# Products of the next panel issued at six norm joints in place of unread products

## The chip, the cores and the metric

The kernel runs on one core of a Trainium2 chip. The metric is the device time of one execution in microseconds; the median of several executions is given. TensorE (PE in the profile) multiplies, VectorE (DVE) and ScalarE (ACT) do elementwise work, SyncE (SP) issues the transfers.

## The reference

Two stacks of transformer blocks on 256 rows of width 1024, in 32-bit floats. What matters here is the sequence of sublayers, each followed by a norm of its 256 x 1024 result, which the next sublayer multiplies by its first weights:

```python
def rmsnorm(x, w):
    y = xf * lax.rsqrt(jnp.mean(xf * xf, axis=-1, keepdims=True) + NORM_EPS)
...
        x = x + hybrid_mixer(rmsnorm(x, norm_mix_w[l]), w_in[l], ...
        x = x + memory_cross_attention(rmsnorm(x, norm_xa_w[l]), rmsnorm(mem, norm_mem_w[l]),
                                       xa_wq[l], xa_wkv[l], xa_wo[l])
        x = x + peer_ffn(rmsnorm(x, norm_ffn_w[l]), peer_wq[l], peer_sub_keys[l], peer_u[l], peer_v[l])
    return rmsnorm(x, norm_final_w)
...
def post_norm(x, sub, g, b):
    return layer_norm(DN_ALPHA * x + sub, g, b)

def swiglu(x, w1, w3, w2):
    return (jax.nn.silu(x @ w1) * (x @ w3)) @ w2
```

The second stack runs, each with a post_norm behind it: swiglu 0, spatial gating, swiglu 2, (keys and values for later, no norm), swiglu 3, sparse attention, swiglu 5.

## The kernel before

**Tiling.** The 256 rows are two row tiles of 128 (`TILES`). Weights stream in slots of 128 x 2048 through a ring of three; a column slot is a panel of 1024 inputs by 256 outputs, held as eight chunks (`DC`) of 128 inputs. Each operand is split into a high part in fp32r (`ScalarE`, a copy) and a low part, the rest (`VectorE`), and a product is three products: high by high, high by low, low by high. Activations stand transposed in `k.xT` (`x_transposed`): chunk by chunk, 128 inputs by 256 rows, with a high and a low plane. A panel is worked off in two halves `j` of 128 outputs: the weights of a chunk and half are the stationary operand, the 256 rows of `k.xT` the moving one.

**A joint with a norm.** The last products of a sublayer end row tile 0 first. `PostNorm` (layer norm, L2684) and `RmsNorm` (L2898) then take each row tile through the same steps: VectorE adds the residual, ScalarE squares with an accumulated sum (L2771, L2955) and takes the root (L2774, L2957), VectorE scales (L2754, L2938) and TensorE turns the tile in eight transposes (`turn_chunks`, L575), two PSUM banks of four; ScalarE writes each bank as high part (`high`, L404) and VectorE the low part (`low`, L409). Signal `highed` counts the high parts: 2 once tile 0 is there, 4 once tile 1 is.

Between the transposes of tile 0 and those of tile 1 TensorE has nothing that is needed. `stand_in` (L581, L584) fills that time with products of the identity by itself that nobody reads: in `RmsNorm.tensor` 4, then 6 once tile 1 is added, then 4 once `rooted` says its root is taken; in `PostNorm.tensor` 3, 7 and 4. After them come the transposes of tile 1: in the same block of the program where a block ends there (`last`, followed by 8 more stand-ins), or, passed on as `turn`, at the head of the next sublayer.

**The next panel.** `high_first` (L341) issues a first panel's products so that those with the rows' high parts come first: after the transposes of tile 1 it waits for `highed` 3, runs the first four chunks of both halves over all 256 rows (L356 with the weights' high part, L359 with their low part), waits for `highed` 4, runs the other four, waits for the low parts and runs the last sixteen (L389). The first slot of the next sublayer is split ahead by `Beginning`, so its weights are there while the norm runs.

**The six joints** are named here by letter: A, the RMS norm before the memory queries (`panels`); B, the RMS norm before the peer queries, where a block ends inside the joint and tile 1 is turned behind it (`TurnedBehind`); C, spatial gating into swiglu 2, a block ends behind the turned tile 1, and swiglu 2 begins with full 512-column products over high and low plane (L3107) and 256-column ones (L3108); D, swiglu 2 into the keys and values; E, swiglu 3 into the attention's queries, a block ends as in C, and `queries` uses `passes` (L398 to L400); F, attention output into swiglu 5.

Order is that of the code: each engine runs its own list and waits only where a semaphore wait is written.

Of the kernel before, what the change touches and what calls it, by code (L numbers as in the profile page):

```python
# [23 lines left out]
ALU = mybir.AluOpType  # L24
# [287 lines left out]
class Before:  # L312


    def __init__(self, splits_eaten, highed=None, written=None, banks_read=(), parts=None, turn=None, ahead=0):
        self.splits_eaten, self.highed, self.written, self.banks_read = splits_eaten, highed, written, banks_read
        self.parts, self.turn, self.ahead = parts, turn, ahead
        self.waited = 0
# [11 lines left out]
    def part(self, pe, m, i):  # L330
# [5 lines left out]
        if value > self.waited:  # L336
            self.waited = value
            pe.wait_ge(self.written[0], value)


def high_first(pe, before, out, operands, x_on_right, apart=False):  # L341
# [22 lines left out]
    if before.turn is None:  # L364
# [47 lines left out]
class Program:  # L412


    def __init__(self, nc, ctx, a):
# [5 lines left out]
        self.before = None  # L421
        self.gains_free = None
# [213 lines left out]
class TurnedBehind:  # L636
# [20 lines left out]
    def before(self):  # L657
        return Before((self.highed, 2), (self.highed, 2), (self.written, 4 - self.lows_from), turn=self.turn, ahead=2)
# [1551 lines left out]
def pick_and_run_experts(k, room):  # L2210
# [8 lines left out]
    with ExitStack() as ctx, k.stage() as block:  # L2219
# [37 lines left out]
        def _(pe):  # L2257
            def panel(m):
# [12 lines left out]
                if m == 0:  # L2271
                    ins = high_first(pe, behind.before(), out, operands, True)
# [411 lines left out]
class PostNorm:  # L2684
# [4 lines left out]
    def __init__(self, k, ctx, split, gains, which, slots, final=False, squares=None, last=False):  # L2689
# [6 lines left out]
        self.begin = None if final else Beginning(k)  # L2696
        self.gains_free = k.gains_free
# [82 lines left out]
    def ends(self):  # L2780

        self.k.before = Before((self.tile_done, 2 * TILES), (self.highed, 4), (self.written, 4), ((self.written, 1),),
                               turn=self.turn_last)
        self.k.gains_free = self.normed

# [3 lines left out]
    def tensor(self, pe):  # L2789
        if self.begin:  # L2790
            turn_chunks(pe, self.k, self.k.x[:, 0, :], 0, self.banks, 4, self.normed)
            stand_in(pe, self.k, 3)
            if self.which != 0:
# [4 lines left out]
            if self.last:  # L2798
                self.turn_last(pe, range(DC))
                stand_in(pe, self.k, 8)  # L2800
# [40 lines left out]
def out_and_norm(k, aT, slots, gains, which, ahead=None):  # L2841


    with ExitStack() as ctx, k.stage() as block:
# [3 lines left out]
        norm = PostNorm(k, ctx, split, gains, which, slots)  # L2848
# [49 lines left out]
class RmsNorm:  # L2898
# [5 lines left out]
    def __init__(self, k, ctx, split, gain, gain_landed, slots, begin, rows):  # L2904
# [7 lines left out]
        self.begin = Beginning(k, None if begin is True else begin)  # L2912
        self.same = begin is True
# [36 lines left out]
    def scalar(self, act):  # L2950
# [13 lines left out]
        self.high(act, 0)  # L2964
        squares(1)
        for b in range(1, 4 if self.same else 2):
# [5 lines left out]
    def tensor(self, pe):  # L2972
        turn_chunks(pe, self.k, self.rows[0], 0, self.banks, 4, self.normed)
        stand_in(pe, self.k, 4)
        pe.wait_ge(self.added, 2)
        stand_in(pe, self.k, 6)
        pe.wait_ge(self.rooted, 2)
        stand_in(pe, self.k, 4)

    def ends(self):  # L2980

        self.k.before = Before((self.tile_done, TILES), (self.highed, 4), (self.written, 4), ((self.written, 1),),
                               turn=self.turn_last)
# [58 lines left out]
def swiglu(k, gains, which, final=False, compress=None):  # L3042
# [10 lines left out]
    with ExitStack() as ctx, k.stage() as block:  # L3053
# [7 lines left out]
        norm = PostNorm(k, ctx, split, gains, which, 3 * UNITS, final, last=compress is not None)  # L3061
# [18 lines left out]
        def bank(u, n):  # L3080

            return 2 * n + (0 if u == 0 and split.before and not compress else 4)
# [4 lines left out]
        def up(pe, u, i):  # L3087
            for n in range(2):
# [12 lines left out]
                if u == 0 and n == 0 and split.before:  # L3101
                    ins = high_first(pe, split.before, out, operands, True, True)
                else:
# [1106 lines left out]
```

## Time and profile before

| | us |
|---|---|
| median of 3 runs | 2235.57 |
| lowest, highest | 2235.31, 2238.03 |
| span of the profiled execution | 2233.5 |
| TensorE busy in it | 2197.0 (98%) |
| VectorE, ScalarE busy | 1568.6 (70%), 1170.0 (52%) |

The profile is of one execution; for it the page gives the span, from the first to the last instruction, and no separate device time. The median of the runs is 2.1 us above this span. TensorE is busy almost all of the span, but busy counts the unread products of the joints as well, so at a joint one has to read what ends the time before the next needed product. Duration in a row is not spacing: products overlap, and the spacing of n equal ones is their common length less one duration, by n - 1.

### The profile page before, as it was taken

Reading aid. Unit: us, or ns where it says so; the run is one execution under the profiler, and the core shown is the slowest. Engines: PE = TensorE matmul, PEld = TensorE weight load, DVE = VectorE, ACT = ScalarE, POOL = GpSimd, SP = SyncE. Lnnn points to the kernel's source line nnn. Section 1 sums busy time; section 2 is a strip of 40 time slices with the busy share of each in tenths; the row PEclk is TensorE's granted clock in tenths of the full one; section 3 lists DMA queues with packets and bytes.
Section 4 is the critical chain, followed back from the end, with each engine's and each line's share of the span. In section 5 each row is a group of like instructions: output and inputs, shape, how many; then the busy total and the mean of one; then the engine's idle time right before and its main releaser. Section 6 shows DMA issues by size and latency. Waiting matters only on the chain. (4 is left out here: it accounts for less than half of the span.)

```text
span 2233.5 us, 37259 instructions
## 1 busy us (share of the span) xinstructions
PE 2197.0 (98%) x14678; PEld 1964.0 (88%) x14678; DVE 1568.6 (70%) x2935; ACT 1170.0 (52%) x2008; POOL 33.9 (2%) x20
## 2 busy tenths in 40 slices
PE   8999999999999999999999999999999999999998
PEld 8987889999999998888888889988889788888887
DVE  7975659999889976666666557766657465776655
ACT  6643454555554455565555455545544544585544
POOL 0100000010000000000000000000000000000000
PEclk9999999999999999999999999999999999999999
DMA  7418425555444456666655556536455655404552
GB/s 275 151 46 189 170 93 174 181 178 170 144 150 143 150 171 192 194 194 193 194 189 212 190 190 240 191 127 232 176 200 191 248 186 192 175 34 175 184 204 97
DMA packets 78310, 389.98 MB, mean 175 GB/s; under 512 B 9771, under 2 KB 12715, under 8 KB 49868
## 3 DMA queue, kind: packets, MB, share of 16 engines
q1 hardware_dynamic: 76684, 383.33, 49.3%
q0 software_dynamic: 1040, 4.19, 1.5%
q8 instruction: 106, 1.74, 0.3%
q14 instruction: 48, 0.39, 0.1%
q10 hardware_dynamic: 432, 0.33, 0.0%
HBM read 382.57 MB, written 5.24 MB: 174 GB/s over the span
## 5 line engine op out<-in xcount | busy, mean ns | idle before, releaser
L256 DVE TENSOR_TENSOR split_slots<-ring,split_slots 128x1024 fp32r<-128x1024 f32 x402 | 475.3, 1227 | 118.4 <-ACT split_slots L247 118.2
L247 ACT ACTIVATE split_slots<-ring 128x1024 fp32r<-128x1024 f32 x402 | 402.3, 1054 | 149.3 <-PE banks L400 123.3
L3107 PE MATMUL banks<-x_transposed,split_slots 128*128 128x512 f32 x1360 | 478.4, 395 | 0.3 <-PEq L464 0.3
L409 DVE SCALAR_TENSOR_TENSOR expert_lo<-ring,expert_hi 128x512 fp32r<-128x512 f32 x512 | 353.4, 697 | 165.7 <-ACT expert_hi L404 164.6
L404 ACT ACTIVATE expert_hi<-ring 128x512 fp32r<-128x512 f32 x512 | 324.0, 634 | 252.5 <-PE banks L400 252.5
L3108 PE MATMUL banks<-x_transposed,split_slots 128*128 128x256 f32 x1360 | 381.5, 281 | 0.0
L3107 PEld LDWEIGHTS banks<-x_transposed,split_slots 128*128 128x128 f32 x1360 | 255.3, 188 | 60.4 <-issue 0.5
L398 PE MATMUL banks<-x_transposed,expert_hi 128*128 128x256 f32 x1024 | 293.9, 287 | 2.5 <-DVE expert_lo L409 2.5
L399 PE MATMUL banks<-x_transposed,expert_hi 128*128 128x256 f32 x1024 | 287.8, 281 | 0.0
L400 PE MATMUL banks<-x_transposed,expert_lo 128*128 128x256 f32 x1024 | 287.7, 281 | 0.0
L3108 PEld LDWEIGHTS banks<-x_transposed,split_slots 128*128 128x128 f32 x1360 | 256.4, 189 | 1.5
L400 PE MATMUL banks<-expert_hi,weighted_split 128*128 128x512 f32 x512 | 199.2, 389 | 0.0
L398 PE MATMUL banks<-expert_hi,weighted_split 128*128 128x512 f32 x512 | 199.2, 389 | 0.0
L399 PE MATMUL banks<-expert_lo,weighted_split 128*128 128x512 f32 x512 | 199.2, 389 | 0.0
L3206 DVE TENSOR_TENSOR gate_and_value<-banks,products_with_low_parts 128x512 f32<-128x512 f32 x88 | 60.8, 691 | 195.8 <-ACT products_with_low_parts L3162 195.8
L398 PEld LDWEIGHTS banks<-x_transposed,expert_hi 128*128 128x128 f32 x1024 | 193.1, 189 | 3.8 <-DVE expert_lo L409 3.2
L399 PEld LDWEIGHTS banks<-x_transposed,expert_hi 128*128 128x128 f32 x1024 | 193.1, 189 | 0.0
L400 PEld LDWEIGHTS banks<-x_transposed,expert_lo 128*128 128x128 f32 x1024 | 193.0, 189 | 0.0
L3162 ACT ACTIVATE products_with_low_parts<-banks 128x512 f32<-128x512 f32 x88 | 52.6, 598 | 237.4 <-PE banks L3108 233.8
L398 PE MATMUL banks<-x_transposed,split_slots 128*128 128x256 f32 x544 | 154.1, 283 | 0.3 <-PEq L464 0.3
L399 PE MATMUL banks<-x_transposed,split_slots 128*128 128x256 f32 x544 | 152.7, 281 | 0.0
L400 PE MATMUL banks<-x_transposed,split_slots 128*128 128x256 f32 x544 | 152.7, 281 | 0.0
(491 smaller groups left out, 4020.5 us busy)
## 6 DMA issues: line engine op xcount, KB each, us to landing
ring<-in_ffn_w SPq DMA_DIRECT2D x132, 1024.0 KB, 4.8
ring<-in_peer_u SPq DMA_DIRECT2D x128, 512.0 KB, 3.5
ring<-in_peer_v SPq DMA_DIRECT2D x128, 512.0 KB, 3.6
ring<-in_w_in SPq DMA_DIRECT2D x16, 1024.0 KB, 6.0
ring<-in_sgu_w_in SPq DMA_DIRECT2D x16, 1024.0 KB, 4.8
ring<-in_peer_wq SPq DMA_DIRECT2D x8, 1024.0 KB, 7.3
ring<-in_sgu_w_out SPq DMA_DIRECT2D x8, 1024.0 KB, 4.9
ring<-in_kv_w SPq DMA_DIRECT2D x6, 1024.0 KB, 4.8
```

Of the source, the lines that this page charges most:

```text
L247: act.activation(self.parts[:, b, 0, p], self.k.w.slot(g)[:, p], ACT.Copy).then_inc(self.high_done, 1)
L256: ins = dve.tensor_tensor(self.parts[:, b, 1, p], self.k.w.slot(g)[:, p], self.parts[:, b, 0, p].bitcast(F32), ALU.subtract)
L398: pe.matmul(out, lh, rh, start=start, stop=False)
L399: pe.matmul(out, lh, rl, start=False, stop=False)
L400: return pe.matmul(out, ll, rh, start=False, stop=stop)
L404: return act.activation(dst, src, ACT.Copy, scale=scale)
L409: return dve.scalar_tensor_tensor(dst, src, scale, hi.bitcast(F32), ALU.mult, ALU.subtract)
L3107: pe.matmul(out(j, slice(0, 2 * SEQ)), lh, k.xT.both[:, c, :, :], start=(c == 0), stop=False)
L3108: ins = pe.matmul(out(j), ll, rh, start=False, stop=(c == DC - 1))
L3162: act.activation(rest[:, n, :, :], sums(u, n, 1), ACT.Copy).then_inc(copied[n], 1)
L3206: dve.tensor_tensor(whole[:, n, :, :], sums(u, n, 0), rest[:, n, :, :], ALU.add).then_inc(joined[n], 1)
```

## The change

A new class `TileAhead` issues products of the next panel for one row tile: for both halves and the asked chunks the weights' high part and low part by the 128 columns of the tile's high part. At each joint, behind the transposes of tile 0 and the first stand-ins (4 in `RmsNorm`, 3 in `PostNorm`), TensorE now waits for the panel's split weights and `highed` 1, issues 16 such products, waits for `highed` 2 and issues 16 more; then it waits for `rooted` 2 and issues 4 stand-ins. The other stand-ins there (6 and 7) are gone. After the transposes of tile 1 the next sublayer issues the same 32 products for tile 1 (A, B, D, F in `high_first`, E in `queries`) where 32 products of 256 columns stood, and at C each pair of 512 and 256 columns becomes one of 384 and one of 128. In `RmsNorm.scalar` the high part of bank 1 moves ahead of the squares of tile 1.

In the core of the diff below the arguments that hand `TileAhead` on (`k.ahead`, `begun`, `apart`) are partly left out.

```diff
+class TileAhead:
...
+    def ready(self, pe):
+        g = self.begin.g
+        pe.wait_ge(self.k.w.used[g % RING], g // RING + 1)
+
+    def products(self, pe, i, chunks=range(DC)):
...
+        rows = slice(i * P, (i + 1) * P)
+        for j in range(2):
+            bank, at = (j, i * P) if self.apart else (0, j * SEQ + i * P)
+            own = slice(j * P, (j + 1) * P)
+            for c in chunks:
+                first = i == 0 and c == 0 and (j == 0 or self.apart)
+                out = k.psum[:, bank, at:at + P]
+                pe.matmul(out, wh[:, c, own], k.xT.hi[:, c, rows], start=first, stop=False)
+                pe.matmul(out, wl[:, c, own], k.xT.hi[:, c, rows], start=False, stop=False)
@@ high_first
-    if before.turn is None:
+    if before.begun:
+        before.turn(pe, near)
+        before.turn(pe, far)
+        pe.wait_ge(before.highed[0], 3 - before.ahead)
+        before.begun.products(pe, 1, near)
+        pe.wait_ge(before.highed[0], 4 - before.ahead)
+        before.begun.products(pe, 1, far)
+    elif before.turn is None:
@@ PostNorm.tensor
             stand_in(pe, self.k, 3)
-            if self.which != 0:
+            if self.ahead:
+                self.ahead.ready(pe)
+                pe.wait_ge(self.highed, 1)
+                self.ahead.products(pe, 0, range(DC // 2))
+                pe.wait_ge(self.highed, 2)
+                self.ahead.products(pe, 0, range(DC // 2, DC))
+                pe.wait_ge(self.rooted, 2)
+                stand_in(pe, self.k, 4, 7)
+            elif self.which != 0:
                 pe.wait_ge(self.negated, 2 * TILES)
                 stand_in(pe, self.k, 7)
@@ RmsNorm.scalar
         self.high(act, 0)
+        self.high(act, 1)
         squares(1)
-        for b in range(1, 4 if self.same else 2):
+        for b in range(2, 4 if self.same else 2):
@@ swiglu, u == 0 and n == 0
+                elif u == 0 and n == 0 and ahead:
+                    rest = k.xT.both.rearrange("p c q n -> p c (q n)")[:, :, P:2 * SEQ]
...
+                            pe.matmul(out(j, slice(P, 2 * SEQ)), lh, rest[:, c, :], start=False, stop=False)
+                            ins = pe.matmul(out(j, slice(P, SEQ)), ll, rh[:, P:SEQ], start=False, stop=(c == DC - 1))
@@ queries
+            if m == 0:
+                ahead.products(pe, 1)
...
+                    if m == 0:
+                        ins = pe.matmul(k.psum[:, 0, j * SEQ:(j + 1) * SEQ], wh[:, c, own], k.xT.lo[:, c, :], start=False,
+                                        stop=(j == 1 and c == DC - 1))
```

In the orders below `split_slots` is the weights' split parts, `x_transposed` is `k.xT`, `ident` the identity, and a bracket names the semaphores that an instruction waits for. TensorE at joint D before, from the end of tile 0's transposes:

```order
L584 MATMUL banks<-ident 128x128 x3
L584 MATMUL banks<-ident 128x128 [waits stage_odd_13]
L584 MATMUL banks<-ident 128x128 x6
L584 MATMUL banks<-ident 128x128 [waits stage_odd_15]
L584 MATMUL banks<-ident 128x128 x3
L3589 UNCONDITIONAL_BRANCH
L575 MATMUL banks<-ident,x_natural 128x128 [waits stage_odd_18,slot_used_2]
L575 MATMUL banks<-ident,x_natural 128x128 x3
L575 MATMUL banks<-ident,x_natural 128x128 [waits stage_odd_18]
L575 MATMUL banks<-ident,x_natural 128x128 x3
L356 MATMUL banks<-x_transposed,split_slots 128x256 [waits stage_odd_20,stage_odd_21]
L359 MATMUL banks<-x_transposed,split_slots 128x256
```

The same place after the change; lines L365 and L366 alternate, 32 times in the first stretch and 32 in the second:

```order
L620 MATMUL banks<-ident 128x128 x3
L365 MATMUL banks<-x_transposed,split_slots 128x128 [waits stage_odd_20,slot_used_2]
L366 MATMUL banks<-x_transposed,split_slots 128x128
...
L365 MATMUL banks<-x_transposed,split_slots 128x128 [waits stage_odd_20]
...
L620 MATMUL banks<-ident 128x128 [waits stage_odd_15]
L620 MATMUL banks<-ident 128x128 x3
L3651 UNCONDITIONAL_BRANCH
L611 MATMUL banks<-ident,x_natural 128x128 [waits stage_odd_18,slot_used_2]
...
L365 MATMUL banks<-x_transposed,split_slots 128x128 [waits stage_odd_20]
...
L424 MATMUL banks<-x_transposed,split_slots 128x256 [waits stage_odd_21]
```

Seven stand-ins that waited for the mean of tile 1 have become 32 products of 128 columns, ahead of the transposes of tile 1; the products behind those transposes are as many as before, 32, and half as wide.

ScalarE at joint A before, from the squares of tile 0:

```order
L2955 ACTIVATE normed_rows,row_stats<-x_natural 128x1024 [waits stage_even_9]
L2957 ACTIVATE row_stats<-row_stats,epsilons 128x1 [waits stage_even_10]
L404 ACTIVATE x_transposed<-banks 128x4x128 [waits stage_even_14]
L2955 ACTIVATE normed_rows,row_stats<-x_natural 128x1024 [waits stage_even_9]
L2957 ACTIVATE row_stats<-row_stats,epsilons 128x1 [waits stage_even_10]
L404 ACTIVATE x_transposed<-banks 128x4x128 [waits stage_even_14] x3
```

and after:

```order
L3003 ACTIVATE normed_rows,row_stats<-x_natural 128x1024 [waits stage_even_9]
L3005 ACTIVATE row_stats<-row_stats,epsilons 128x1 [waits stage_even_10]
L439 ACTIVATE x_transposed<-banks 128x4x128 [waits stage_even_14] x2
L3003 ACTIVATE normed_rows,row_stats<-x_natural 128x1024 [waits stage_even_9]
L3005 ACTIVATE row_stats<-row_stats,epsilons 128x1 [waits stage_even_10]
L439 ACTIVATE x_transposed<-banks 128x4x128 [waits stage_even_14] x2
```

One high part has moved ahead of the squares of tile 1.

## Rows read from the trace of the kernel before

**Rows 1.** Busy times; waits of TensorE: us, times, longest us.
```profile
PE 2197.0 (98%) x14678; PEld 1964.0 (88%) x14678; DVE 1568.6 (70%) x2935; ACT 1170.0 (52%) x2008; POOL 33.9 (2%) x20
PE banks L356 <- ACT x_transposed L404: 1.0, 5, 0.2
PE banks L584 <- DVE norm_stats L2745: 0.9, 4, 0.3
```

**Rows 2.** Timeline of TensorE, joint D: start us, length us, engine, line, work.
```profile
1688.71 1.04 PE L575 MATMUL banks<-ident,x_natural 128*128 128x128 f32 x8
1689.58 0.83 PE L584 MATMUL banks<-ident 128*128 128x128 f32 x6
1690.64 2.76 PE L584 MATMUL banks<-ident 128*128 128x128 f32 x22 [0.23 <-DVE norm_stats L2745]
1693.40 1.23 PE L575 MATMUL banks<-ident,x_natural 128*128 128x128 f32 x8
1694.81 0.36 PE L356 MATMUL banks<-x_transposed,split_slots 128*128 128x256 f32 x1 [0.18 <-ACT x_transposed L404]
```

**Rows 3.** Stand-ins (L584) by window, A to F: first stand-in : first transpose, length, busy.
```profile
258.01:261.20 3.19, 3.19 (x28) 1.00 0.00 0
326.34:330.97 4.63, 3.29 (x28) 1.00 0.00 0
1496.68:1500.44 3.76, 3.50 (x28) 1.00 0.00 0
1689.58:1693.40 3.82, 3.59 (x28) 1.00 0.00 0
1932.54:1936.27 3.73, 3.50 (x28) 1.00 0.00 0
2037.28:2041.03 3.75, 3.59 (x28) 1.00 0.00 0
```

**Rows 4.** Timeline of TensorE: spacing of 512-column, 256-column and identity products.
```profile
900.05 0.39 PE L398 MATMUL banks<-expert_hi,weighted_split 128*128 128x512 f32 x1
...
901.87 0.39 PE L400 MATMUL banks<-expert_hi,weighted_split 128*128 128x512 f32 x1
...
336.18 2.06 PE L389 MATMUL banks<-x_transposed,split_slots 128*128 128x256 f32 x16
338.07 0.28 PE L398 MATMUL banks<-x_transposed,split_slots 128*128 128x256 f32 x1
...
326.34 3.29 PE L584 MATMUL banks<-ident 128*128 128x128 f32 x28
```

**Rows 5.** Weight loads by shape: line, stationary partitions * columns, count, busy us, mean ns.
```profile
L359 PEld LDWEIGHTS banks<-x_transposed,split_slots 128*128 128x128 f32 x112 | 21.1, 189 | 0.0
L400 PEld LDWEIGHTS banks<-x_transposed,narrow_split 128*48 128x48 f32 x8 | 1.0, 122 | 0.0
L400 PEld LDWEIGHTS banks<-x_transposed,gate_panel_split 128*16 128x16 f32 x8 | 0.8, 95 | 0.2
```

**Rows 6.** Timelines of weight loads and products, 117.5 to 118.5 us: 16 and 32 columns.
```profile
117.69 0.30 PEld L1037 LDWEIGHTS banks<-log_alpha_f,constants_sb 128*128 128x128 f32 x2
117.91 0.30 PEld L1038 LDWEIGHTS banks<-log_alpha_f,constants_sb 128*128 128x128 f32 x2
118.14 0.30 PEld L1039 LDWEIGHTS banks<-log_by_half,ones 128*128 128x128 f32 x2
...
117.80 0.29 PE L1037 MATMUL banks<-log_alpha_f,constants_sb 128*128 128x16 f32 x2
```

**Rows 7.** Timeline of ScalarE and VectorE, joint B.
```profile
326.11 0.60 ACT L404 ACTIVATE x_transposed<-banks 128x512 fp32r<-128x512 f32 x1 [3.30 <-PE banks L575]
326.93 1.06 ACT L2955 ACTIVATE first_blocks<-x_natural 128x1024 f32<-128x1024 f32 x1 [0.23 <-DVE x_natural L2930]
...
329.97 0.68 DVE L409 SCALAR_TENSOR_TENSOR x_transposed<-banks,x_transposed 128x512 fp32r<-128x512 f32 x1
```

**Rows 8.** Timeline of TensorE, behind joints C and E.
```profile
1501.59 1.95 PE L584 MATMUL banks<-ident 128*128 128x128 f32 x16
1503.84 0.47 PE L3107 MATMUL banks<-x_transposed,split_slots 128*128 128x512 f32 x1 [0.30 <-PEq L464]
...
1946.29 0.32 PE L398 MATMUL banks<-x_transposed,narrow_split 128*48 128x256 f32 x1 [0.71 <-DVE narrow_split L409]
```

More of the change, by code:

```diff
@@ L421, in __init__ @@
         self.before = None
+        self.ahead = None
         self.gains_free = None
@@ L655, in lows, with before @@
             split_low(dve, self.k.xT.lo[bank_part(b)], bank4(self.k, 4 + b), self.k.xT.hi[bank_part(b)]).then_inc(self.written, 1)
-    def before(self):
-        return Before((self.highed, 2), (self.highed, 2), (self.written, 4 - self.lows_from), turn=self.turn, ahead=2)
+    def before(self, begun=None):
+        return Before((self.highed, 2), (self.highed, 2), (self.written, 4 - self.lows_from), turn=self.turn, ahead=2,
+                      begun=begun)
 def bank4(k, b):
@@ L2271, in panel @@
                 if m == 0:
-                    ins = high_first(pe, behind.before(), out, operands, True)
+                    ins = high_first(pe, behind.before(k.ahead), out, operands, True)
                 else:
@@ L2684, with __init__ @@
 class PostNorm:
-    def __init__(self, k, ctx, split, gains, which, slots, final=False, squares=None, last=False):
+    def __init__(self, k, ctx, split, gains, which, slots, final=False, squares=None, last=False, apart=None):
         self.last = last
@@ L2696, in __init__ @@
         self.begin = None if final else Beginning(k)
+        self.ahead = None if apart is None else TileAhead(k, self.begin, apart)
         self.gains_free = k.gains_free
@@ L2912, in __init__ @@
         self.begin = Beginning(k, None if begin is True else begin)
+        self.ahead = TileAhead(k, self.begin, False)
         self.same = begin is True
@@ L2974, in tensor @@
         stand_in(pe, self.k, 4)
-        pe.wait_ge(self.added, 2)
-        stand_in(pe, self.k, 6)
+        self.ahead.ready(pe)
+        pe.wait_ge(self.highed, 1)
+        self.ahead.products(pe, 0, range(DC // 2))
+        pe.wait_ge(self.highed, 2)
+        self.ahead.products(pe, 0, range(DC // 2, DC))
         pe.wait_ge(self.rooted, 2)
-        stand_in(pe, self.k, 4)
+        stand_in(pe, self.k, 4, 7)
     def ends(self):
         self.k.before = Before((self.tile_done, TILES), (self.highed, 4), (self.written, 4), ((self.written, 1),),
-                               turn=self.turn_last)
+                               turn=self.turn_last, begun=self.ahead)
+        self.k.ahead = None if self.same else self.ahead
 def out_and_rms_norm(k, aT, slots, gain, gain_landed, begin, rows=None):
@@ L3060, in swiglu @@
         copied, joined = ([k.sig.new() for _ in range(2)] for _ in range(2))
-        norm = PostNorm(k, ctx, split, gains, which, 3 * UNITS, final, last=compress is not None)
+        ahead = None if split.before else k.ahead
+        norm = PostNorm(k, ctx, split, gains, which, 3 * UNITS, final, last=compress is not None,
+                        apart=False if which in (2, 3) else None)
         if compress:
@@ L3080, in bank @@
         def bank(u, n):
-            return 2 * n + (0 if u == 0 and split.before and not compress else 4)
+            return 2 * n + (0 if u == 0 and (split.before or ahead) and not compress else 4)
         def sums(u, n, q):
@@ L3276, in spatial_gating @@
          mixed, biased, gated, high, low) = (k.sig.new() for _ in range(16))
-        norm = PostNorm(k, ctx, split, gains, 1, slots, squares=v[:, :, 0:D], last=True)
+        norm = PostNorm(k, ctx, split, gains, 1, slots, squares=v[:, :, 0:D], last=True, apart=True)
         def mixed_by(m):
@@ L3703, in query_and_attend @@
         rows.before = None
+        ahead = k.ahead
         narrow = k.sb(ctx, "narrow_panel", [P, DC, WIDTH])
```

27 lines of the change are left out of this document (19 added, 8 removed).

## The prediction

> **What bounds the kernel now.** I read the busy times first: TensorE is busy 98% of the span, VectorE 70%, ScalarE 52% [rows 1]. Then its waits, which are small at the joints: 1.0 us in five places for the high part of tile 1, 0.9 us in four for a mean [rows 1]. So time goes only where TensorE's own list becomes shorter, or where what it now does for nobody becomes work. The timeline at joint D shows how much of the latter there is [rows 2]: transposes of tile 0 at 1688.71, stand-ins from 1689.58, transposes of tile 1 at 1693.40, first needed product at 1694.81. From the first stand-in to the transposes of tile 1 a joint has 3.19 to 3.82 us, in B 4.63 with the end of a block in it [rows 3]. The chain on VectorE and ScalarE sets the end of this time, and the stand-ins are cut to it. The question is whether what replaces them fits, and what it takes off behind. Everything hangs on one price: the spacing m of fp32r products with 128 columns, of which the trace has none.
>
> **The price m.** Eight products of 512 columns take 901.87 - 900.05 = 1.82 us, 0.228 each; sixteen of 256 take 338.07 - 336.18 = 1.89, 0.118 each [rows 4]. The line through both gives 0.063 us at 128 columns and 0.173 at 384. That is the lower bound. But each product also loads new weights, and the load does not shrink with the moving columns. Loads of 16, 48 and 128 weight columns of fp32r operands (the profile writes f32 for these too) last 95, 122 and 189 ns [rows 5]: 94 ns more for 112 columns, 0.84 ns a column, so 128 columns stream for 107 ns. A product of 256 columns hides this, one of 128 does not. The nearest rows for back-to-back loads with short products are the 32-bit products of 16 and 32 columns at 117.7 us: pairs of loads begin at 117.69, 117.91 and 118.14, so 0.1125 us a load though only 16 columns move [rows 6]. I take m between this 0.1125 and the 0.118 of 256 columns, at 0.115: half the columns for nearly the whole price. An upper bound is the 32-bit product of 128 columns, which runs as two records of 3.19/28 = 0.114 us each [rows 3], 0.228 together.
>
> The Trainium skill, TensorE: Matmul & The Clock Gate, section LDWEIGHTS, says that a load takes its weight columns divided by 1.2 ns, however deep it is, which makes 107 ns for 128 columns; rows 5 agree. It speaks against this change, whose products load as much as before for half the work.
>
> **Before the transposes of tile 1.** After the change TensorE issues a stand-ins (4 in A and B, 3 elsewhere; each is two records, so 0.91 or 0.68 us), 32 products for tile 0, and 4 stand-ins behind the wait for the root (0.91). With m = 0.115 the products take 3.68 us.
> - A: 0.91 + 3.68 + 0.91 = 5.50, against 3.19 [rows 3]: +2.31.
> - C, D, E, F: 0.68 + 3.68 + 0.91 = 5.27, against 3.76, 3.82, 3.73, 3.75 [rows 3]: +1.51, +1.45, +1.54, +1.52.
> - B: the block ends 0.32 us after VectorE's low part, 329.97 + 0.68 = 330.65 [rows 7], for the transposes start at 330.97 [rows 3]. After, TensorE is last: 326.34 + 5.50 = 331.84, and 0.17 more until its last product has ended (0.28 long at a spacing of 0.11 [rows 4]), 332.01, and transposes at 332.33: +1.36.
>
> The root is long taken by then, so the last four stand-ins cover nothing and are all cost. Other new waits hide: in B the first high part is there at 326.11 + 0.60 = 326.71 [rows 7], before the products could start at 327.25; the second follows 0.6 us later, while the first sixteen take 1.84. The removed waits for means were 0.9 us in all [rows 1] and lie in the windows above. Moving the second high part ahead of the squares in A and B delays these from 326.93 to 327.31 [rows 7], by 0.38; TensorE is later than that by itself, so it costs nothing now, and 0.38 where the products are cheap. The granted clock is 1.00 in all six windows [rows 3], its upper level, 2.4 GHz, and TensorE stays as busy, so I add nothing for the clock.
>
> **Behind them.** The way from the first transpose of tile 1 to the first product, 1694.81 - 1693.40 = 1.41 us in D [rows 2], is transposes, a high part and their delays, and stays.
> - A, B, D, F: 32 products of 128 columns for 32 of 256: 32 x (0.115 - 0.118) = -0.10 each. The low parts, queued behind on VectorE, are due only when they end.
> - C: its second four transposes no longer wait for the scaling, for both halves are long there: 8 x 0.11, the spacing of 28 stand-ins, (3.29 - 0.28)/27 [rows 4], instead of 1501.59 - 1500.44 [rows 3, 8], -0.25. The block end then passes 1.26 on. Swiglu 2 begins with 16 pairs of 384 and 128 columns for 16 of 512 and 256: 16 x (0.173 + 0.115 - 0.228 - 0.118) = -0.93.
> - E: the same -0.25 at the transposes, so 1.29 comes through the block end. In `queries` 0.10 is saved, but behind it TensorE waits 0.71 us for the narrow panel's low part [rows 8], whose chain starts at the block's start. So the 0.10, and whatever a cheap m would give here, is lost in that wait.
>
> **The sum.** A 2.21, B 1.26, C 0.33, D 1.35, E 1.29, F 1.42: +7.9 us. The profiled span of 2233.5 becomes 2241.4; the median of the runs is 2.1 above the span, and 2235.57 + 7.9 = 2243.4. The sum holds 336 m (64 in A, B, D, F, 48 in C, 32 in E), so 1 ns of m is 0.34 us: m = 0.1125 gives +7.0, 0.118 gives +8.9, 0.107 gives +5.2, and 0.14, a load that overlaps badly, +16.3. It breaks even at 0.115 - 7.9/336 = 0.0915.
>
> **The rivals.**
> *Half the price (faster).* Loads are pulled so far ahead that two overlap, and m is the 0.063 of the line. Then 0.68 + 2.02 + 0.91 = 3.61 fits in C to F [rows 3], A is 0.65 late, B 0.38 (VectorE). Behind: -1.76 in A, B, D, F (32 x 0.055) and in C (16 x 0.110), nothing in E. Sum: -1.11 - 1.38 - 1.76 - 1.76 - 1.76 = -7.8, 2227.8 us. It decides where m is under 0.0915. For it: the line is good between 512 and 256, and the stand-ins would then just fill the gap. Against: 0.1125 a load in rows 6.
> *Between.* Load and product overlap in part and m lies halfway from 0.063 to 0.107, 0.085: 7.9 - 336 x 0.030 = -2.2, 2233.4, no change one can tell. No row supports it.
> The Trainium skill, same page, section Back-to-back issue gap, states 81 ns sustained for load and product pairs of 128 columns; by it the sum would be 7.9 - 336 x 0.034 = -3.5, 2232.1 us. Rows 6 speak against it for 32-bit weights; its chance is that of this case.
> *Priced like 32-bit (much slower).* Narrow fp32r products run like plain 32-bit ones, m = 0.228 [rows 3]: 336 x 0.113 = +38.0, and in E 3.52 more less the 0.71 of its wait, +2.8. With 7.9 it is +48.7, 2284.3 us. For it: no fp32r product under 256 columns exists in this trace to exclude it. Against: fp32r and 32-bit loads look alike, and fp32r needs one record a product where 32-bit needs two [rows 4].
> *In series.* Load and product do not overlap, 0.107 + 0.063 = 0.170: +18.5, and 0.9 in E, 2262.9 us. Against: 256 columns would then cost 0.225, not 0.118.
>
> **How the numbers follow.** Forecast 0.68, half price 0.07, between 0.06, like 32-bit 0.16, in series 0.03. The forecast's own span is 2239 to 2252 (m from 0.107 to 0.14, with 1 us for my joins of the timelines). The range takes in the cases below it too, 2226 to 2252, which holds 0.81; the two much slower cases are left out with 0.19. What a measurement can tell from no change is about 0.2%, 4.5 us. Faster by more: half price and a bit of between, 0.08. Within: the rest of between and 0.07 of the forecast's low end, 0.12. Slower: 0.80.
>
> **What would show it.** In the profile after, the products of line 365 and 366 at a spacing near 0.115 us, with about 3.7 us for each 32; the four stand-ins behind them without a wait before them; the transposes of tile 1 at D 5.3 us after the first stand-in, and the first product still 1.4 us after those; at B the block end led by TensorE; at E a wait of 0.7 to 0.8 us before the narrow panel. A spacing near 0.063, and a wait for the scaling before the transposes at C to F, would prove me wrong towards faster; two records for one product, or 7 us for 32, towards much slower.

## The result and the profile after

| | before | after |
|---|---|---|
| median, us | 2235.86 | 2241.76 |
| lowest, highest | 2234.92, 2238.03 | 2240.92, 2243.55 |
| executions | 10 | 10 |
| span of the profiled execution | 2233.5 | 2238.9 |

The kernel after takes 1.0025 times as long as the kernel before, with a 95% interval of 1.0017 to 1.0033: slower by 5.9 us in the medians and by 5.4 in the spans. The prediction said 7.9, with a range for the time of 2226 to 2252 us. The direction and the mechanism were right, and the size was 2 us too large.

The busy times of the kernel after, to be held against [rows 1]:

```profile
PE 2203.5 (98%) x14790; PEld 1973.6 (88%) x14790; DVE 1569.4 (70%) x2935; ACT 1169.4 (52%) x2008; POOL 33.9 (2%) x20
```

TensorE has 112 more records and is busy 6.5 us more. VectorE and ScalarE are as busy as before, within 0.8 us. The change works on TensorE alone, and the groups of its instructions by line and shape show what came in (columns: busy us, mean ns of one, idle time before them and what ended it):

```profile
L365 PE MATMUL banks<-x_transposed,split_slots 128*128 128x128 f32 x176 | 40.3, 277 | 1.3 <-ACT x_transposed L439 1.0 <-PEq L500 0.3
L366 PE MATMUL banks<-x_transposed,split_slots 128*128 128x128 f32 x176 | 39.9, 274 | 0.0
...
L620 PE MATMUL banks<-ident 128*128 128x128 f32 x206 | 26.7, 277 | 1.0 <-PEq L500 1.0
...
L3163 PE MATMUL banks<-x_transposed,split_slots 128*128 128x384 f32 x16 | 4.7, 389 | 0.3 <-PEq L500 0.3
...
L3164 PE MATMUL banks<-x_transposed,split_slots 128*128 128x128 f32 x16 | 3.6, 222 | 0.0
```

There are 352 of the narrow products of lines 365 and 366, each one record long. The stand-ins (L620) are 206 records where they were 286. A product of 128 columns lasts 277 or 274 ns among its own kind (L365, L366) and 222 ns behind one of 384 columns (L3164). This difference is taken up again below.

The timeline of TensorE at joint D after the change, to be held against [rows 2] (start us, length us, line, work):

```profile
1691.37 1.03 PE L611 MATMUL banks<-ident,x_natural 128*128 128x128 f32 x8
1692.24 0.83 PE L620 MATMUL banks<-ident 128*128 128x128 f32 x6
...
1692.83 0.31 PE L365 MATMUL banks<-x_transposed,split_slots 128*128 128x128 f32 x1
...
1696.44 1.11 PE L620 MATMUL banks<-ident 128*128 128x128 f32 x8
1697.38 1.04 PE L611 MATMUL banks<-ident,x_natural 128*128 128x128 f32 x8
...
1698.67 0.33 PE L365 MATMUL banks<-x_transposed,split_slots 128*128 128x128 f32 x1 [0.25 <-ACT x_transposed L439]
...
1702.29 2.10 PE L424 MATMUL banks<-x_transposed,split_slots 128*128 128x256 f32 x16
```

In the kernel before, the stretch ends where its line 389 starts:

```profile
1698.67 2.06 PE L389 MATMUL banks<-x_transposed,split_slots 128*128 128x256 f32 x16
```

Read both as differences of starts.

| joint D, us | before | after |
|---|---|---|
| stand-ins ahead of the products for tile 0 | | 1692.83 - 1692.24 = 0.59 |
| 32 products for tile 0 | | 1696.44 - 1692.83 = 3.61 |
| four stand-ins | | 1697.38 - 1696.44 = 0.94 |
| first stand-in to the transposes of tile 1 | 3.82 | 5.14 |
| these transposes to the first product | 1.41 | 1698.67 - 1697.38 = 1.29 |
| 32 products behind it | 1698.67 - 1694.81 = 3.86 | 1702.29 - 1698.67 = 3.62 |

That 1698.67 stands in both columns is chance: it is the start of line 389 before and of the first product of tile 1 after. Thirty-two products of 128 columns take 3.61 us, and thirty-two of 256 columns took 3.86 with the small wait for the second high part in them. The 64 narrow products take 7.23 us together, 3.37 more than the 32 wide ones. The gap of 3.82 us had room for 2.29 of it, for the stand-ins that stay take 0.59 and 0.94. So the gap grew by 3.61 - 2.29 = 1.32, and 0.12 + 0.24 came back behind it.

The same reading at all six joints gives the next table. It has the gap from the first stand-in to the transposes of tile 1, and what a joint cost in all. For that the lag of after behind before is taken at the transposes of tile 0 of one joint and of the next; for F at the end of the span.

| joint | gap before | gap after | forecast of the gap | joint in all | forecast |
|---|---|---|---|---|---|
| A | 3.19 | 5.36 | 5.50 | +1.93 | +2.21 |
| B | 4.63 | 5.82 | 5.99 | +1.02 | +1.26 |
| C | 3.76 | 5.13 | 5.27 | +0.03 | +0.33 |
| D | 3.82 | 5.14 | 5.27 | +0.84 | +1.35 |
| E | 3.73 | 5.13 | 5.27 | +1.12 | +1.29 |
| F | 3.75 | 5.14 | 5.27 | +0.78 | +1.42 |

The joints add up to +5.72. Ahead of joint A the kernel after was 0.32 us ahead in its profiled execution, where the change touches nothing. Together it makes 5.4. Two executions differ by more than that where nothing was changed: the profiled one of the fourth experiment below runs the same instructions as before up to C, and there the transposes of tile 0 come at 1498.58 instead of 1495.79, 2.8 us later. So an entry that spans the whole way from one joint to the next can be off by as much. Read only inside the joint, from the transposes of tile 0 to the first work behind them that is the same in both kernels, the six cost 1.92, 0.97, -0.03, 1.01, 1.12 and 1.07 us, 6.06 together. The joints hold the whole loss.

### The profile page after: what moved, and what is told of

Read it like the earlier page. It is cut to its first block and busy times, and to the rows that moved or that the text cites. A ratio compares the mean times of both kernels' runs of the same rounds, so it can differ in the third digit from the quotient of the medians.

```text
span 2238.9 us, 37486 instructions
## 1 busy us (share of the span) xinstructions
PE 2203.5 (98%) x14790; PEld 1973.6 (88%) x14790; DVE 1569.4 (70%) x2935; ACT 1169.4 (52%) x2008; POOL 33.9 (2%) x20
## 5 line engine op out<-in xcount | busy, mean ns | idle before, releaser
L3169 PE MATMUL banks<-x_transposed,split_slots 128*128 128x512 f32 x1344 | 472.2, 395 | 0.0
L3170 PE MATMUL banks<-x_transposed,split_slots 128*128 128x256 f32 x1344 | 376.9, 280 | 0.0
L3169 PEld LDWEIGHTS banks<-x_transposed,split_slots 128*128 128x128 f32 x1344 | 252.4, 188 | 58.9
L3170 PEld LDWEIGHTS banks<-x_transposed,split_slots 128*128 128x128 f32 x1344 | 253.4, 189 | 1.5
L433 PE MATMUL banks<-x_transposed,split_slots 128*128 128x256 f32 x528 | 149.5, 283 | 0.0
L434 PE MATMUL banks<-x_transposed,split_slots 128*128 128x256 f32 x528 | 148.2, 281 | 0.0
L435 PE MATMUL banks<-x_transposed,split_slots 128*128 128x256 f32 x528 | 148.2, 281 | 0.0
```

The source lines that it names most:

```text
L433: pe.matmul(out, lh, rh, start=start, stop=False)
L434: pe.matmul(out, lh, rl, start=False, stop=False)
L435: return pe.matmul(out, ll, rh, start=False, stop=stop)
L3169: pe.matmul(out(j, slice(0, 2 * SEQ)), lh, k.xT.both[:, c, :, :], start=(c == 0), stop=False)
L3170: ins = pe.matmul(out(j), ll, rh, start=False, stop=(c == DC - 1))
```

## The experiments

Every verdict here is against the kernel before, run on the same chip beside it. There it had medians of 2235.97 (27 executions) for the first four kernels and 2236.47 (13) for the last.

The theory is that a product costs as much as the load of the next weights where it streams for less time than that load, so that half the columns cost nearly the whole price. The rivals are that narrow fp32r products have a price of their own, that the last stand-ins or the delayed squares of the RMS norm are to blame, and that the narrow products are cheap but something else is late.

### The price of one product, by moving and by stationary columns

```diff
             norm.tensor(pe)
+            if final:
+                probe(pe)
...
+            def one(c, cols, n):
+                pe.matmul(k.psum[0:cols, 6 + c % 2, 0:n], w[:, c % DC, 0:cols], x[:, 0:n], start=True, stop=True)
+            for c in range(24):
+                one(c, 128, 256)
...
+            for c in range(24):
+                one(c, 32, 128)
+            for c in range(24):
+                one(0, 128, 128)
```

> The kernel before, with nine stretches of 24 unread products each put behind the last needed product on TensorE: fp32r operands, stationary columns x moving columns 128x256, 128x192, 128x128, 128x64, 64x256, 64x128, 64x64, 32x128, and 128x128 with the same weights named each time. Theory (the load of the stationary operand sets the spacing of narrow products): 128x256 0.118 us, then 128x192, 128x128 and 128x64 all 0.1125, the same again with the weights named each time; 64x256 0.118, 64x128 and 64x64 about 0.06 (the load halves), 32x128 0.06. Rival (narrow fp32r products stream at two cycles a column): 64x128 and 32x128 stay at 0.11, 128x64 and 64x64 fall to 0.06, 128x192 is 0.17. The time itself is longer by what of the 21 us does not hide under the last norm and says nothing.

The kernel with the probe at its end had 2248.39 us in its one timed execution. The time says only that the products are there; the timeline has the prices. Each line is one window of TensorE within the nine groups of 24, in the order in which they were issued. "128*64" are stationary partitions by stationary columns, "128x256" ends in the moving columns.

```profile
2226.33 1.45 PE L3134 MATMUL banks<-hidden,x_transposed 128*128 128x256 f32 x11
...
2228.74 1.50 PE L3134 MATMUL banks<-hidden,x_transposed 128*128 128x192 f32 x12
...
2231.50 1.39 PE L3134 MATMUL banks<-hidden,x_transposed 128*128 128x128 f32 x11
...
2234.14 1.50 PE L3134 MATMUL banks<-hidden,x_transposed 128*128 128x64 f32 x12
...
2237.01 1.46 PE L3134 MATMUL banks<-hidden,x_transposed 128*64 128x256 f32 x11
...
2239.19 1.18 PE L3134 MATMUL banks<-hidden,x_transposed 128*64 128x128 f32 x17
...
2240.48 1.21 PE L3134 MATMUL banks<-hidden,x_transposed 128*64 128x64 f32 x18
...
2241.89 1.19 PE L3134 MATMUL banks<-hidden,x_transposed 128*32 128x128 f32 x17
...
2244.16 1.50 PE L3134 MATMUL banks<-hidden,x_transposed 128*128 128x128 f32 x12
```

The spacing is the length less one duration, divided by the count less one. The group of 128 moving columns has a duration of 0.274, so it gives (1.39 - 0.274) / 10 = 0.112 us.

| moving columns | 128 stationary | 64 stationary | 32 stationary |
|---|---|---|---|
| 256 | 0.117 | 0.118 | |
| 192 | 0.112 | | |
| 128 | 0.112 | 0.060 | 0.060 |
| 64 | 0.111 | 0.058 | |
| 128, the same weights each time | 0.112 | | |

With 128 stationary columns the price does not depend on the moving columns from 192 down to 64. Halve the stationary columns, and a product of 128 moving columns falls from 0.112 to 0.060, while one of 256 stays where it was. Both sides are needed for the verdict: the narrow product is not slow by its shape, it is held by the load of its weights. From 64 to 32 stationary columns the 0.060 stays. Here the load no longer matters, and the streaming of the 128 columns is left, near the 0.063 at which the prediction's line puts it. The weight loads of the same trace fit (line, stationary partitions * columns, count, busy us, mean ns):

```profile
L3134 PEld LDWEIGHTS banks<-hidden,x_transposed 128*128 128x128 f32 x120 | 13.8, 191 | 0.1
L3134 PEld LDWEIGHTS banks<-hidden,x_transposed 128*64 128x64 f32 x72 | 5.7, 136 | 0.0
L3134 PEld LDWEIGHTS banks<-hidden,x_transposed 128*32 128x32 f32 x24 | 1.5, 109 | 0.0
```

From 64 to 128 stationary columns a load lasts 55 ns longer, and a product of 64 moving columns costs 53 ns more. Naming the same weights each time saves nothing, and the count says why: 120 loads of 128 columns are those of all five groups, the last one's 24 among them.

The rival of the prediction at m = 0.063 and the case between at 0.085 fall here, and so does a price like that of 32-bit products. The break-even of 0.0915 lies between the price with 128 stationary columns and that with 64. Stationary operands half as wide are no way out: they need twice as many products, and 2 x 0.060 is more than 0.112.

The Trainium skill, TensorE: Matmul & The Clock Gate, section LDWEIGHTS, says that a load takes its weight columns divided by 1.2 ns, by which an estimate is 107 ns for 128 and 53 ns for 64. The measured 0.112 and 0.058 us lie 5 ns above it. The section Back-to-back issue gap of the same page gives 81 ns sustained for load and product at 128 columns. For these fp32r operands the measurement, 0.112, decides against it.

### Without the last four stand-ins

```diff
@@ TileAhead's place in PostNorm.tensor and RmsNorm.tensor
                 self.ahead.products(pe, 0, range(DC // 2, DC))
-                pe.wait_ge(self.rooted, 2)
-                stand_in(pe, self.k, 4, 7)
```

> The changed kernel without the four stand-ins and the wait for the root behind the tile 0 products, at all six joints. Theory (the loss is that the products for tile 0 and these stand-ins overhang the chain on VectorE and ScalarE): in the trace of the changed kernel the four take 0.95 us a joint. All of it goes at A, C, D, E, F, at B 0.84, where VectorE then ends the block. That is -5.5 us against the changed kernel, 2236.3, the same as before within what can be measured. Rival (they are covered by the chain, and the loss is behind the joints, in the next panel): no change against the changed kernel, 2241.8.

Measured: 2236.74 us (2235.62 to 2238.15, 10 executions), ratio to before 1.000, interval 0.9991 to 1.001. The kernel after was at 2241.76 beside a before of 2235.86, so 24 unread stand-ins were worth 5.0 us, or 5.1 if each is taken against its own before: 0.84 to a joint. The timeline of TensorE at A and D:

```profile
257.27 1.03 PE L611 MATMUL banks<-ident,normed_rows 128*128 128x128 f32 x8
...
262.56 1.06 PE L611 MATMUL banks<-ident,normed_rows 128*128 128x128 f32 x8
...
1689.39 1.03 PE L611 MATMUL banks<-ident,x_natural 128*128 128x128 f32 x8
...
1694.46 1.06 PE L611 MATMUL banks<-ident,x_natural 128*128 128x128 f32 x8
```

From the transposes of tile 0 to those of tile 1 it is 5.29 us at A and 5.07 at D. After the change it was 6.24 (A, 256.82 to 263.06) and 6.01 (D). The transposes of tile 1 start without a wait, as soon as the 32 products are through. So nothing but these products stands in front of them, and the four stand-ins covered no wait. The two gaps are shorter by 0.95 and 0.94, which would make 5.6 us at six joints where the medians give 5.0; no run tells whether the rest is more than the scatter of executions.

### Without the first ones too

```diff
@@ PostNorm.tensor
-            stand_in(pe, self.k, 3)
+            if not self.ahead:
+                stand_in(pe, self.k, 3)
@@ RmsNorm.tensor
-        stand_in(pe, self.k, 4)
         self.ahead.ready(pe)
```

> As no_trailing, and also without the three (PostNorm) or four (RmsNorm) stand-ins ahead of the tile 0 products. Theory: these cover the time until the first high part is there, which is all but 0.24 us at C to F and 0.37 at A; at B VectorE ends the block, so nothing. -1.3 us against no_trailing, 2235.0, not to be told from before. If a joint fell to a lower granted clock without them, the next panel would show it in its rows, and the time would be some us above no_trailing.

Measured: 2235.39 us (2234.89 to 2236.76, 10 executions), ratio 0.9996, interval 0.9987 to 1.0006. The timeline of TensorE at A, C and F:

```profile
261.60 1.06 PE L611 MATMUL banks<-ident,normed_rows 128*128 128x128 f32 x8
...
1496.10 1.04 PE L611 MATMUL banks<-ident,x_natural 128*128 128x128 f32 x8
...
1497.48 0.30 PE L365 MATMUL banks<-x_transposed,split_slots 128*128 128x128 f32 x1 [0.33 <-ACT x_transposed L439]
...
2035.97 1.04 PE L611 MATMUL banks<-ident,x_natural 128*128 128x128 f32 x8
...
2047.83 0.40 PE L3165 MATMUL banks<-x_transposed,split_slots 128*128 128x512 f32 x1
```

At C the first product waits 0.33 us for the first high part, and it does so 1.38 us after the transposes, where with three stand-ins it was 1.46 (at D, 1692.83 - 1691.37). So the first stand-ins were a cover after all: 0.59 us of them lay beside a wait and hid all but 0.1 of their own price. At A the gap shrank by 0.32, from 5.29 to 4.97. Taking these 20 stand-ins away gave 1.35 us in the medians, near the expected 1.3, but not by its terms: 0.24 was expected at each of C to F, and the traces show 0.09 to 0.10 there, 0.8 at all six joints. The agreement is in part luck. The granted clock is 1.00 at all six joints of this kernel, so the stand-ins were not needed for it.

The 24 last and 20 first stand-ins together are 6.4 us, and the change had cost 5.9. So the loss is as large as the unread work that the kernel after kept, and without that work the products break even.

At F it is 2047.83 - 2035.97 = 11.86 us from the transposes of tile 0 to the first full panel. Before it was 11.79, with all its stand-ins: the next panel starts at 2048.20 in its timeline, and the transposes at 2036.41. The idea in its cleanest form, with no unread work left at this joint and 64 needed products of 128 columns in place of 32 of 256, brings nothing there: 32 of these products take 3.6 us, and the gap was 3.75.

### At two joints only, with fewer products behind

This is the kernel before with the change at C and F alone and without stand-ins around it. At F the products behind the transposes of tile 1 are 34 instead of 48. The weights' high part meets the high rows of tile 1 and the low rows of both in one product of 384 columns, as C does it.

```diff
@@ high_first, at F
+                    pe.matmul(out(j, slice(P, SEQ)), ll, rh[:, P:SEQ], start=False, stop=False)
+        before.rows_low(pe)
...
+            for c in range(1, DC):
+                (lh, ll), (rh, rl) = operands(j, c)
+                ins = pe.matmul(out(j, slice(P, 2 * SEQ)), lh, both[:, c, :], start=False, stop=(c == DC - 1))
```

> The kernel before with the change at C and F alone, where the low plane has columns of its own, without stand-ins around the tile 0 products; at F the products behind the turned tile are 16 low-weight ones of 128 columns, then per half one of 128 and one of 256 for chunk 0 and seven of 384 columns, 34 in all in place of 48. Theory (a product narrower than its load saves nothing, one of 384 for 512 saves its columns): C +0.2 before the transposes and -1.0 behind, F +0.2 and -0.1 before, -1.0 behind, sum -1.9 us against before: 2234.0. Rival (whatever is saved in a first panel is lost at the next wait of that sublayer): 2236.2, no gain.

Measured: 2234.13 us (2233.45 to 2236.59, 11 executions), ratio 0.9991, interval 0.9982 to 1.000. The median lies 1.8 us under before, near the expected 2234.0; the interval just reaches no change. The timeline of TensorE at C and F:

```profile
1498.58 1.05 PE L623 MATMUL banks<-ident,x_natural 128*128 128x128 f32 x8
...
1511.31 0.44 PE L3174 MATMUL banks<-x_transposed,split_slots 128*128 128x512 f32 x1
...
2038.47 1.04 PE L623 MATMUL banks<-ident,x_natural 128*128 128x128 f32 x8
...
2046.88 1.39 PE L409 MATMUL banks<-x_transposed,split_slots 128*128 128x384 f32 x7
...
2049.56 0.39 PE L3174 MATMUL banks<-x_transposed,split_slots 128*128 128x512 f32 x1
```

The same ends in the kernel before, and then in the kernel after:

```profile
1509.57 0.39 PE L3107 MATMUL banks<-x_transposed,split_slots 128*128 128x512 f32 x1
...
2048.20 0.40 PE L3107 MATMUL banks<-x_transposed,split_slots 128*128 128x512 f32 x1
```

```profile
1512.17 0.44 PE L3169 MATMUL banks<-x_transposed,split_slots 128*128 128x512 f32 x1
...
2053.89 0.39 PE L3169 MATMUL banks<-x_transposed,split_slots 128*128 128x512 f32 x1
```

| transposes of tile 0 to the first full work, us | before | after | no stand-ins | two joints |
|---|---|---|---|---|
| C, to the seventeenth pair of the first panel | 1509.57 - 1495.79 = 13.78 | 1512.17 - 1498.42 = 13.75 | | 1511.31 - 1498.58 = 12.73 |
| F, to the next panel | 2048.20 - 2036.41 = 11.79 | 2053.89 - 2041.03 = 12.86 | 11.86 | 2049.56 - 2038.47 = 11.09 |

In these stretches C gains 1.05 us and F 0.70, together 1.75, where the medians differ by 1.84. The profiled execution was the longest of the eleven, 2236.59, so only stretches inside a joint are compared here, not its starts or its span. Line 409 shows why F differs from the same joint without stand-ins: seven products of 384 columns, each 0.338 us long, stand at (1.39 - 0.338) / 6 = 0.175 us. So 128 needed columns ride along in a wide product for 0.06 us more than the 0.118 of 256 columns, where they cost 0.112 alone. Fourteen of them are 0.77 us, which is 11.86 - 11.09.

### The second high part ahead of the squares, alone

```diff
@@ RmsNorm.scalar, in the kernel before
         self.high(act, 0)
+        self.high(act, 1)
         squares(1)
-        for b in range(1, 4 if self.same else 2):
+        for b in range(2, 4 if self.same else 2):
```

> The kernel before with one edit of the change alone: in the RMS norm, ScalarE writes the high part of bank 1 ahead of the squares of tile 1 (joints A and B). Nothing is left out or added. Theory: the prediction said that this delays the squares by 0.38 us and that TensorE feels it only where its own work ends before them. In the kernel before TensorE has stand-ins there, so the delay shows: transposes of tile 1 at A come 0.3 to 0.4 us later behind those of tile 0 than before (4.06 us there), at B 0.2 to 0.4 later, 2236.3 to 2236.7 us in all. In the kernel without the unread products TensorE reached tile 1 at A 4.97 us behind tile 0, later than the 4.4 that this allows, so the edit costs nothing there. Rival: the squares are not on the chain at all and the transposes stay where they were, 2235.9.

Measured: 2236.29 us (2235.78 to 2237.08, 10 executions), ratio 0.9999, interval 0.9989 to 1.0008. The timelines of ScalarE and TensorE at A:

```profile
258.08 1.08 ACT L404 ACTIVATE x_transposed<-banks 128x512 fp32r<-128x512 f32 x2 [3.30 <-PE banks L575]
259.05 1.06 ACT L2955 ACTIVATE normed_rows<-x_natural 128x1024 f32<-128x1024 f32 x1
...
257.44 1.03 PE L575 MATMUL banks<-ident,normed_rows 128*128 128x128 f32 x8
...
261.66 1.23 PE L575 MATMUL banks<-ident,normed_rows 128*128 128x128 f32 x8
```

The squares start 259.05 - 257.44 = 1.61 us behind the transposes of tile 0, where they started 1.46 behind them in the kernel before, and the transposes of tile 1 come 4.22 behind instead of 4.06. At B it is 5.65 instead of 5.50. The theory had the sign of it, since the squares are on the chain where TensorE has only stand-ins. But it had the size wrong: 0.15 us to a joint, under the expected 0.3 to 0.4 at A and 0.2 to 0.4 at B, and too little for the medians to show. The rival, that nothing moves, fits the median and not the trace.

The prediction's 0.38 added the lengths of two high parts, 326.11 + 0.60 + 0.60 = 327.31 [rows 7]. On ScalarE, too, length is not spacing: the two high parts last 1.08 together, and the squares start 259.05 - 258.08 = 0.97 us behind the first one. Before, they started 0.83 behind it, with a wait of 0.23 for VectorE's addition in between:

```profile
257.77 0.60 ACT L404 ACTIVATE x_transposed<-banks 128x512 fp32r<-128x512 f32 x1 [3.29 <-PE banks L575]
258.60 1.06 ACT L2955 ACTIVATE normed_rows<-x_natural 128x1024 f32<-128x1024 f32 x1 [0.23 <-DVE x_natural L2930]
```

So the second high part fills this wait and pushes the squares only by what is left of it, 0.14.

## Why the prediction came out as it did

**The price m** decided everything, and its step held. It was bracketed by a load of 16 to 32 moving columns, 0.1125, and by a product of 256 columns, 0.118, and the argument was that the load does not shrink with the moving columns. The measured m is 3.60 / 32 = 0.1125 at A (258.51 to 262.11) and 0.112 in the probe. The middle of the bracket, 0.115, was a choice without a reason: with the load as the bound, the row of short products back to back was the nearest one, if of 32-bit weights, and its 0.1125 should have been taken. This mis-sized term is 336 x 0.0025 = 0.84 us of the 2.2 that the sum was over.

**The gap** was forecast 0.13 to 0.17 too long at every joint, 0.85 in all. Of the 0.14 or so at a joint, 0.08 is m (32 x 0.0025) and counts in the 0.84 above. The first stand-ins took 0.59 or 0.81 where 0.68 or 0.91 stood, 0.09 to 0.10 too much. The 0.114 a record was the whole gap of [rows 3] over its count, which is more than the spacing in the same rows, (3.29 - 0.28) / 27 = 0.1115. That is under 0.02 of it. Another 0.04 lies in how the first product is recorded: at D it starts at 1692.83 and the next at 1692.98, so 0.04 us of the stretch stands in its own 0.31. For the 0.03 that is left there is no row. The last four took 0.94 to 0.95 where 0.91 stood, 0.03 the other way. They cost their full price, as forecast. There was no wait before them, and the run without them gave 5.0 us back where the sum had 6 x 0.91 = 5.5.

**B.** The end of the block is led by TensorE, as forecast: the transposes come 5.82 us after the first stand-in, against 5.99.

**The way from the transposes to the first product** was to stay 1.41 and became 1.29 at D, and 1.28 at A and F. This step failed in kind, if only by 0.12 us to a joint. The eight transposes of [rows 2] are 1.23 long at D and those after are 1.04. In the kernel before they ran close behind the scaling of tile 1 and had to wait inside the group for its second half. After, the scaled rows have long been there. The prediction used this very effect at C and E and overlooked it at A, D and F. At B there was nothing to gain, for the end of the block stands between the scaling and the transposes; the way is 1.32 before and 1.31 after.

**Behind them** 32 x (0.115 - 0.118) = -0.10 was forecast, and D shows 3.62 for 3.86, -0.24. Of these, 0.18 is m, and the rest lies in the first products, where before also waited for the second high part.

**C.** The term was +0.33 and 0.03 came. The transposes were to give 0.25 and gave 0.27 (1505.31 - 1504.43 against 1501.59 - 1500.44). The sixteen pairs were to give 0.93 and gave 1.11, for they took 1512.17 - 1507.55 = 4.62 us, and 1509.57 - 1503.84 = 5.73 before. The pair before cost 5.73 / 16 = 0.358, not 0.346: 0.43 for the first and 0.353 for each of the others, and no run shows why. Here the mis-sized term is the work that went away. The pair's price after, 4.62 / 16 = 0.289, is what was put in, 0.173 + 0.115, and the experiments have 0.175 for 384 columns among their own kind and 0.112 for 128, 0.287 together. TensorE's timeline at C after the change:

```profile
1507.55 0.41 PE L3163 MATMUL banks<-x_transposed,split_slots 128*128 128x384 f32 x1 [0.30 <-PEq L500]
1507.81 0.22 PE L3164 MATMUL banks<-x_transposed,split_slots 128*128 128x128 f32 x1
1507.87 0.39 PE L3163 MATMUL banks<-x_transposed,split_slots 128*128 128x384 f32 x1
1508.09 0.22 PE L3164 MATMUL banks<-x_transposed,split_slots 128*128 128x128 f32 x1
1508.15 0.39 PE L3163 MATMUL banks<-x_transposed,split_slots 128*128 128x384 f32 x1
```

From the start of a product of 384 columns to that of the next narrow one it is 0.22 us, and only 0.06 from there to the next wide one. The weights of the narrow product were loaded beside the wide one, and those of the wide one had only the narrow product to hide beside. This stall stands in the record of the product that waits for its weights: the wide one lasts 389 ns, and the narrow one 222, against 274 to 277 among its own kind. Among their own kind products of 384 columns last 338, as the kernel with the change at two joints shows (count, shortest, median and longest in ns):

```profile
L409 PE MATMUL banks<-x_transposed,split_slots x14: 333/338/339, 2046.9 to 2049.4; 128*128 128x384 f32 x14
```

So the stall has only moved from the narrow record to the wide one. The narrow product looks like 0.06 us there, but it makes the pair 0.289 - 0.175 = 0.114 dearer than the wide product alone, which is its price among its own kind.

**E.** The term was +1.29, and +1.12 came. That anything saved in the queries is lost in front of the narrow panel shows in the timeline of TensorE there:

```profile
1950.91 0.32 PE L433 MATMUL banks<-x_transposed,narrow_split 128*48 128x256 f32 x1 [0.92 <-DVE narrow_split L444]
```

The wait was 0.71 in [rows 8] and is 0.92 now, 0.21 more. The cheaper products and the quicker start ended up there, as forecast for 0.10 of it: from the first product of the block to the narrow panel it is 6.63 us before and 6.62 after.

**D and F** cost 0.84 and 0.78 where 1.35 and 1.42 stood. At D the terms above make 1.32 - 0.12 - 0.24 = 0.96, so 0.39 of the difference is theirs. At F the stretch from the transposes of tile 0 to the next panel lost 1.07, so 0.35 is theirs, and 0.29 comes later, where the change has no part. That remainder is as large as the 0.32 ahead of A, within what two executions differ by, and no run settles whether it has a cause.

**The delayed squares** were said to cost nothing after the change, because TensorE is later by itself, and 0.38 where it is not. The last experiment has them worth 0.15 us at a joint where TensorE has only stand-ins. In the kernel without stand-ins the transposes of tile 1 at A come 261.60 - 256.63 = 4.97 us after those of tile 0, beyond the 4.22 at which the delayed chain would allow them. So they are covered even there.

**The rivals.** Half the price and the case between needed m under 0.0915; priced like 32-bit needed 0.228 and two records; in series needed 0.170. The probe excludes all four. No granted clock moved: its mean is 0.999 before and after, and it is 1.00 at all six joints of both, the upper level of 2.4 GHz.

## What to carry to other kernels

Price a product by the longer of two times, its own streaming and the load of the next stationary operand; with 128 stationary columns of fp32r the second is 0.112 us, which still binds at 192 moving columns and no longer at 256. Splitting a product by rows to start half of it earlier then costs nearly the whole product again, and it pays only where the idle gap is longer than that (here 3.6 us for 32) and nothing unread is left in it. Let a narrow rest ride along in a wide product where it can: as part of one, 128 columns cost 0.06. As a product of their own behind a wide one they still cost 0.11, for a pair of 384 and 128 columns takes 0.289 where 384 alone take 0.175. That the next record starts 0.06 behind the narrow one says nothing of its price.

## What the runs showed of the hardware that the rows before could not show

- With 128 stationary fp32r columns the spacing is flat, at 0.112, 0.112 and 0.111 us for 192, 128 and 64 moving columns. With 64 stationary columns it is 0.060 and 0.058 for 128 and 64.
- Products that name the same weights one after another cost as much as with new ones, 0.112 us: the probe has 24 loads for the 24 of them.
- The stall for a load stands within the record of a product, 277 ns against 222 for the same 128 columns and 389 against 338 for the same 384. So the busy share of TensorE rises with it, and the trace shows no wait.
- A pair of 384 and 128 columns takes 0.289 us, 0.114 more than a product of 384 columns among its own kind, at 0.175.
